# Router products token-major in step with the LayerNorm, and the first expert gather split between the first weight rows

## The reference, cut to what matters

```python
def moe_swiglu(x, w_router, b_router, wg, wu, wd):
    xt = x.reshape(B * T, D_MODEL)
    logits = (xt @ w_router).astype(jnp.float32) + b_router.astype(jnp.float32)
    vals, idx = lax.top_k(logits, TOP_K)              # TOP_K = 2 of N_EXPERTS = 8
    wts = jax.nn.softmax(vals, axis=-1)
    gate = jnp.sum(jax.nn.one_hot(idx, N_EXPERTS, dtype=jnp.float32) * wts[..., None], axis=1)
    for e in range(N_EXPERTS):                         # D_FF_EXPERT = 1408
        out = out + gate[:, e:e + 1] * swiglu(xt, wg[e], wu[e], wd[e])
```

## Time and profile before

| | us |
|---|---|
| median of three runs | 1650.25 (1649.96 to 1652.37) |
| the profiled execution | 1651.5 |
| its span, first to last instruction | 1649.7 |
| PE busy in the span | 1520.7 (92%) |
| DVE, ACT, POOL busy | 1077.6, 853.0, 555.4 |

### The profile page before, as it was taken

The page is one execution under the profiler, slowest core; times in us unless marked ns, Lnnn a source line. Parts: engine busy times, 40 slices in busy tenths (PEclk is TensorE's granted clock), DMA queues, the critical chain, the costliest instruction groups (busy, mean ns, idle before and its releaser), DMA issues. The chain is left out here.

```text
span 1649.7 us, 23014 instructions
## 1 busy us (share of the span) xinstructions
PE 1520.7 (92%) x8707; PEld 1339.8 (81%) x8707; DVE 1077.6 (65%) x1546; ACT 853.0 (52%) x1472; POOL 555.4 (34%) x336
## 2 busy tenths in 40 slices
PE   7999799999799999799998998996999999999995
PEld 6789799787699999678898988973788888888774
DVE  6779786658611011467887855777477877787784
ACT  4656555532433233355565635313566676576673
POOL 0036543000376567300555520010233343343342
PEclk9999899989899999999998998897799999999998
DMA  6322124312355455053322333125387987798780
GB/s 245 128 77 92 63 77 133 128 52 96 128 165 167 118 152 166 1 182 103 103 78 77 100 118 120 55 80 206 126 302 284 330 314 289 256 358 319 266 328 33
DMA packets 57523, 264.66 MB, mean 160 GB/s; under 512 B 9024, under 2 KB 9664, under 8 KB 48448
## 3 DMA queue, kind: packets, MB, share of 16 engines
q1 hardware_dynamic: 57408, 263.11, 45.9%
HBM read 254.54 MB, written 8.54 MB: 159 GB/s over the span
## 5 line engine op out<-in xcount | busy, mean ns | idle before, releaser
L1020 PE MATMUL ps<-Xh,Wl 128*128 128x320 f32 x976 | 332.0, 340 | 26.2 <-DVE Wl L1816 14.6
L1938 DVE TENSOR_TENSOR ml<-mraw,mh 128x1408 fp32r<-128x1408 f32 (+1 forms) x160 | 291.4, 1854 | 75.9 <-ACT mh L901 75.9
L901 ACT ACTIVATE mh<-mraw 128x1408 fp32r<-128x1408 f32 (+1 forms) x216 | 268.0, 1253 | 112.9 <-PE ps L1342 110.9
L1021 PE MATMUL ps<-Xl,Wh 128*128 128x320 f32 x976 | 312.9, 321 | 0.0
L1022 PE MATMUL ps<-Xh,Wh 128*128 128x320 f32 x976 | 312.7, 320 | 0.0
L555 POOL TENSOR_TENSOR cacc<-cacc,G 128x320 f32<-128x320 f32 x180 | 192.5, 1069 | 350.4 <-ACT G L681 334.3
L583 POOL TENSOR_TENSOR ml<-mraw,mh 128x1408 fp32r<-128x1408 f32 (+1 forms) x56 | 178.7, 3192 | 320.3 <-ACT mh L901 320.3
L1020 PEld LDWEIGHTS ps<-Xh,Wl 128*128 128x128 f32 x976 | 193.9, 199 | 50.4 <-issue 29.2
L1816 DVE TENSOR_TENSOR Wl<-raw,Wh 128x1024 fp32r<-128x1024 f32 x138 | 174.9, 1268 | 75.9 <-ACT Wh L610 74.9
L1021 PEld LDWEIGHTS ps<-Xl,Wh 128*128 128x128 f32 x976 | 194.4, 199 | 0.3
L1022 PEld LDWEIGHTS ps<-Xh,Wh 128*128 128x128 f32 x976 | 193.6, 198 | 0.0
(11 more groups left out here) (336 smaller groups left out, 2953.4 us busy)
## 6 DMA issues: line engine op xcount, KB each, us to landing
mraw<-w_moe SPq DMA_DIRECT2D x128, 704.0 KB, 6.7
raw<-w_mix SPq DMA_DIRECT2D x68, 1024.0 KB, 4.9
mraw<-w_moe SPq DMA_DIRECT2D x88, 512.0 KB, 4.7
fraw<-w_ffn SPq DMA_DIRECT2D x44, 512.0 KB, 3.5
fraw<-w_ffn SPq DMA_DIRECT2D x16, 704.0 KB, 4.0
Ss<-st_delta SPq DMA_DIRECT2D x2, 2048.0 KB, 9.4
o_delta_s<-Ss SPq DMA_DIRECT2D x8, 512.0 KB, 2.6
X<-x SPq DMA_DIRECT2D x2, 640.0 KB, 5.6
```

The costliest lines, as they stand in the source:

```text
L901: act.activation(mh[:, n % MS, 0:w], mraw[:, n % MRAW, 0:w], ACT.Copy).then_inc(m_hi, 1)
L1020: pe.matmul(out, wl, xh, start=start, stop=False)
L1021: pe.matmul(out, wh, xl, start=False, stop=False)
L1938: dve.tensor_tensor(ml[:, n % MS, 0:w], mraw[:, n % MRAW, 0:w], mh[:, n % MS, 0:w].bitcast(f32), ALU.subtract).then_inc(m_lod, 1)
```

## The change

1. **Router.** For each tile of `X`, PE makes the scores with the tile as the stationary operand, 128 tokens by 8 experts in three groups of tokens, and then turns the same tile's three groups. The copy of the scores on ACT and the turning of the scores are gone. The copies to `xth` go by halves of the width.
2. **Rests of the rows 0, 1 and 2** go to POOL (`pooled`), and `mlo(0)` to `mlo(2)` fall away on DVE.
3. **Places.** `slot` counts from 1, and `posm` is 0 where a token did not choose: the subtractions and the fill with -1 are gone, two products take the place of six instructions. PE signals the places before it makes the totals. `places` is two `tensor_tensor` comparisons for both experts of a pair, in place of six `tensor_scalar`. The flag is set after the first `places`.
4. **First gather.** The four parts of it are each gathered from `xth` and `xtl` together; two parts precede row 0, the third follows row 0 and the fourth follows row 1. `xtl` is made in two halves around `places`. `gate_weights`, the start of `acc` and `slots` move into the rows of expert 0.

```diff
         def pooled(n):
-            return n % MN in MPOOL
+            return n % MN in MPOOL or n < 3
...
             def router(l):
-                eight(wrt, PS[6], shifts(l, 2) - KT, rt_made)
...
+                for k in range(KT):
+                    pe.wait_ge(aff_done, shifts(l, 2) - KT + k + 1)
+                    for t in range(3):
+                        ins = pe.matmul(PS[7][0:rows(t), 8 * t:8 * t + 8], X[:, k, cols(t)], wrt[:, k, :],
+                                        start=(k == 0 and t == 0), stop=(k == KT - 1), skip_group_check=True)
+                    if k == KT - 1:
+                        ins.then_inc(rt_done, 1)
+                    for t in range(3):
+                        ins = pe.transpose(PS[3 * (k // 4) + t][0:rows(t), 128 * (k % 4):128 * (k % 4) + 128], X[:, k, cols(t)],
+                                           C("ident"))
+                        if k % 4 == 3:
+                            ins.then_inc(xt_mm, 1)
...
+                def gather_first(n):
...
+                    gather(PS[7 if n % 2 == 0 else 5], xth, 0, n)
+                    if n == 0:
+                        pe.wait_ge(xt_dve, 3)
+                        pe.wait_ge(flag_made, 1)
+                    gather(PS[6 if n % 2 == 0 else 4], xtl, 0, n)
+
+                gather_first(0)
+                gather_first(1)
...
+                        if not e and k < 2:
+                            gather_first(k + 2)
-                        if k == 2:
+                        if k == (2 if e else 5):
...
-                mlo(0)
-                mlo(1)
+                dve.memset(posm[:, :, :], 0.0)
                 dve.wait_ge(rt_done, 1)
...
+                x_rest(0)
                 dve.wait_ge(pos_done, 1)
...
+                dve.tensor_tensor(posm[:, 0:2, 0:NE], PS[7][:, 0:16].rearrange("p (t e) -> p t e", t=2), rk[:, 3, 0:2, :], ALU.mult)
+                link(dve.tensor_tensor(posm[0:64, 2, 0:NE], PS[7][0:64, 16:24], rk[0:64, 3, 2, :], ALU.mult))
...
-                    for t in range(3):
-                        ins = dve.tensor_scalar(Pm[:, e // 2 % 2, t, e % 2, :], C("slot"), posm[:, t, e:e + 1], None,
-                                                ALU.is_equal)
-                    ins.then_inc(m_p, 1)
+                    for t, n, r in ((0, 2, 128), (2, 1, 64)):
+                        ins = dve.tensor_tensor(
+                            Pm[0:r, e // 2 % 2, t:t + n, :, :],
+                            C("slot", r).unsqueeze(1).unsqueeze(1).broadcast_to([r, n, 2, CAP]),
+                            posm[0:r, t:t + n, e:e + 2].unsqueeze(3).broadcast_to([r, n, 2, CAP]), ALU.is_equal)
+                    ins.then_inc(m_p, 2)
...
+                    if n == 2:
+                        gate_weights()
+                    if n == 7:
+                        acc_start(l)
```

More of the change, by code:

```diff
@@ L905, in experts @@
                 for q in range(6):
-                    t, half = divmod(q, 2)
+                    half, t = divmod(q, 3)
                     act.wait_ge(xt_mm, q + 1)
@@ L913, in experts, with gathered_first @@
                 mhead(3)
[L914 to L918, removed]
+                def gathered_first(n):
+                    act.wait_ge(m_g, 2 * n + 1)
+                    act.activation(xeh[:, 0, 2 * n:2 * n + 2, :],
+                                   PS[7 if n % 2 == 0 else 5][:, :].rearrange("p (k n) -> p k n", k=2), ACT.Copy)\
                         .then_inc(m_xea, 1)
+                gathered_first(0)
+                gathered_first(1)
                 def gathered(e, n):
@@ L942, in experts @@
                         mhead(n + 3)
+                    if n in (1, 2):
+                        gathered_first(n + 1)
                     if i == MG - 1:
@@ L1275, in experts @@
                     for s in range(t + 1):
-                        pe.matmul(PS[7][0:rows(t), 8 * t:8 * t + 8],
-                                  C("upto", rows(s))[:, 0:rows(t)] if s == t else ones(rows(s), rows(t)),
-                                  rk[0:rows(s), 3, s, :], start=(s == 0), stop=(s == t))
+                        ins = pe.matmul(PS[7][0:rows(t), 8 * t:8 * t + 8],
+                                        C("upto", rows(s))[:, 0:rows(t)] if s == t else ones(rows(s), rows(t)),
+                                        rk[0:rows(s), 3, s, :], start=(s == 0), stop=(s == t))
+                ins.then_inc(pos_done, 1)
                 for s in range(3):
-                    ins = pe.matmul(PS[7][:, 32:40], ones(rows(s)), rk[0:rows(s), 3, s, :], start=(s == 0), stop=(s == 2))
+                    ins = pe.matmul(PS[6][:, 0:8], ones(rows(s)), rk[0:rows(s), 3, s, :], start=(s == 0), stop=(s == 2))
                 ins.then_inc(pos_done, 1)
@@ L1343, in wide @@
                     ins.then_inc(m_done, 1)
[L1345 to L1350, removed]
+                def gather_first(n):
+                    if n == 0:
+                        pe.wait_ge(m_p, 2)
+                        pe.wait_ge(xt_act, 3)
+                    elif n == 1:
+                        pe.wait_ge(xt_act, 6)
+                        pe.wait_ge(xt_dve, 6)
+                    else:
+                        pe.wait_ge(m_xea, n - 1)
+                        pe.wait_ge(m_xev, n - 1)
+                    gather(PS[7 if n % 2 == 0 else 5], xth, 0, n)
+                    if n == 0:
+                        pe.wait_ge(xt_dve, 3)
[3 more added lines that the diff above has]
+                gather_first(1)
                 for e in range(NE):
                     h = slice(CAP * (e % 2), CAP * (e % 2) + CAP)
-                    if e <= NE - 2:
+                    if 1 <= e <= NE - 2:
                         pe.wait_ge(m_xea, XA0 + 2 * e)
@@ L1362, in experts @@
                     for k in range(8 + SCAT):
+                        if not e and k < MG and k % 2 == 0:
+                            pe.wait_ge(m_xea, k // 2 + 1)
+                            pe.wait_ge(m_xev, k // 2 + 1)
                         if k < MG:
@@ L1896, in router @@
                 link(dve.memset(rk[:, :, :, :], 0.0))
-                mlo(0)
-                mlo(1)
+                dve.memset(posm[:, :, :], 0.0)
                 dve.wait_ge(rt_done, 1)
-                for t in range(3):
-                    ins = dve.tensor_tensor(lg[0:rows(t), t, :], PS[7][0:rows(t), 8 * t:8 * t + 8], brt[0:rows(t), :], ALU.add)
-                link(ins)
+                dve.tensor_tensor(lg[:, 0:2, :], PS[7][:, 0:16].rearrange("p (t e) -> p t e", t=2), over(brt[:, :], 2), ALU.add)
+                link(dve.tensor_tensor(lg[0:64, 2, :], PS[7][0:64, 16:24], brt[0:64, :], ALU.add))
                 le = lg.unsqueeze(3).broadcast_to([128, 3, NE, NE])
@@ L1941, in experts, with x_rest @@
             def experts(l):
-                mlo(2)
-                dve.wait_ge(pos_done, 1)
[L1945 to L1952, removed]
-                def places(e):
-                    for t in range(3):
-                        ins = dve.tensor_scalar(Pm[:, e // 2 % 2, t, e % 2, :], C("slot"), posm[:, t, e:e + 1], None,
-                                                ALU.is_equal)
-                    ins.then_inc(m_p, 1)
+                def x_rest(half):
+                    for t in range(3):
+                        q = 3 * half + t
+                        s = slice(512 * half, 512 * half + 512)
+                        dve.wait_ge(xt_act, q + 1)
+                        dve.tensor_tensor(xtl[0:rows(t), t, s], PS[q][0:rows(t), :], xth[0:rows(t), t, s].bitcast(f32),
+                                          ALU.subtract).then_inc(xt_dve, 1)
+                x_rest(0)
+                dve.wait_ge(pos_done, 1)
+                dve.tensor_tensor(posm[:, 0:2, 0:NE], PS[7][:, 0:16].rearrange("p (t e) -> p t e", t=2), rk[:, 3, 0:2, :], ALU.mult)
+                link(dve.tensor_tensor(posm[0:64, 2, 0:NE], PS[7][0:64, 16:24], rk[0:64, 3, 2, :], ALU.mult))
+                def places(e):
+                    for t, n, r in ((0, 2, 128), (2, 1, 64)):
[4 more added lines that the diff above has]
+                    ins.then_inc(m_p, 2)
                 def gathered(e, n):
@@ L1979, in experts, with gathered_first @@
                 places(0)
[L1980 to L1993, removed]
+                dve.wait_ge(pos_done, 2)
+                link(dve.tensor_reduce(rk[:, 1, 0, 0:1], PS[6][:, 0:8], AX.X, ALU.max))
+                dve.tensor_scalar(flag[:, :], rk[:, 1, 0, 0:1], CAP + 0.5, None, ALU.is_gt).then_inc(flag_made, 1)
+                x_rest(1)
+                def gathered_first(n):
+                    dve.wait_ge(m_g, 2 * n + 2)
+                    dve.tensor_copy(xel[:, 2 * n:2 * n + 2, :],
+                                    PS[6 if n % 2 == 0 else 4][:, :].rearrange("p (k n) -> p k n", k=2)).then_inc(m_xev, 1)
+                gathered_first(0)
+                gathered_first(1)
                 for n in range(MT):
```

27 lines of the change are left out of this document (8 added, 19 removed).

## The result

The changed kernel takes 1656.88 us (median of 8 runs, 1653.11 to 1662.38), the kernel before beside it 1650.96 (8 runs, 1649.05 to 1655.33): ratio 1.0038, 95% interval 1.0025 to 1.0050. It is slower by about 6 us; the forecast was 1654.0, slower by 0.23%. The profiled execution of the changed kernel took 1655.09, its span is 1653.0.

The account below looks back on a forecast made before the run. The path to the experts' stage, where PE is busy 423.62 of 430 us, was taken as the bound; 5.0 + 5.1 - 1.9 + 1.7 - 6.1 = +3.8 us on 1650.25 gave 1654.0, range 1648 to 1658.5.

Parts of the forecast that it names:

- rests on POOL under the LayerNorm: Second layer's LayerNorm tail: the two first `scaled` each wait for a POOL rest, so the router starts later, +5.0 us.
- router, from its first product to the scores: PE's new router: nine instructions a tile at clock 0.50, 1.7 us each, eight tiles 13.0 us; +5.1 us.
- from the scores to `Pm`: Choice, three `xtl` rests hiding the places, and two `posm` products take 4.7 us against 6.58: -1.9 us.
- `Pm` to the gather: Both `Pm` comparisons on DVE wait for POOL's rests of rows 2 and 3, ready after 5.6 us: +1.7 us.
- gather to row 6: Gather and first rows: row 0 raises the clock, so parts 3, 4 and row 1 run fast, 24.5 against 30.6: -6.1 us.
- a pair in the first layer: First-layer evidence: two `scaled` took 4.05 us beside two POOL rests of 4.90 us, against 1.02 undisturbed.
- The reason given for the clock: Router on PE: over 4 us idle already, 9 with the delay, so it starts at 0.50, with no reason to rise.
- the stream in the earlier trace: Nearest row for router prices: 128x128 weights, 16 columns, about 0.11 us each at 1.00, then 0.20 to 0.21 at 0.50.
- the comparison's form: `Pm` without waits: six `tensor_scalar` cost about 1.1 us, two `tensor_tensor` some 0.95, by the rows.
- The prediction's other reckoning: `Pm` by the two-elements-a-cycle rule: the new comparisons cost an estimated 0.4 us more, total about 4.3 instead of 3.8.
- the third rival: First rows: the clock does not rise in row 0, +3.8 us more, 1658; chance 0.14.
- The base: Starting time: profiled execution 1651.5 us, taken as 1.25 above the runs' median of 1650.25.

Follow-up runs that it names:

- e0_after: The changed kernel run again unedited: 1657.60 us, 1.0037 of the kernel before.
- e1: The changed kernel with the rests of rows 0 and 1 back on DVE, made while it waits for the scores: 1652.72 us.
- e8: The changed kernel with nine unused 128 by 512 products in PE's idle time ahead of the router: 1654.87 us.
- e10: The changed kernel with rests 0 and 1 on DVE, rows 2 and 3 split later, and four unused products ahead of the router: 1645.82 us.
- e4: The changed kernel with the router of before, its scores copied on ACT and turned afterwards: 1652.27 us.
- e2: The changed kernel with ACT splitting rows 2 and 3 only after moving the gather's first part: 1652.58 us.
- e6: The kernel before with the new router only: 1658.58 us, slower by 0.40%.
- e5: The changed kernel with all four parts of the first gather ahead of row 0: 1661.22 us.
- e7: The changed kernel with the old router, rests 0 and 1 on DVE, and rows 2 and 3 split later: 1640.45 us.
- e9: e7 with three unused products of 256 columns between the router and the gather: 1641.64 us.

## Why the prediction was right, point by point

The direction and the mechanisms held, that of the clock in part; the sum came out small by about 2 of 6 us. Its terms, from the dates in the table (changed, first profile, less before):

| step | forecast | measured |
|---|---|---|
| rests on POOL under the LayerNorm | +5.0 | +4.96 |
| router, from its first product to the scores | +5.1 | +5.95 |
| from the scores to `Pm` | -1.9 | -1.64 |
| `Pm` to the gather | +1.7 | +1.49 |
| gather to row 6 | -6.1 | -6.34 (-5.2 in e0_after, mean of the ten profiles that split it -5.7) |
| sum | +3.8 | +4.4 (+5.5 in e0_after) |

- **Rests on POOL under the LayerNorm.** As forecast, to 0.04 us, and e1 takes the whole of it back. What was read off a pair in the first layer carried over.
- **Router.** The term that was mis-sized: 1.80 us a tile, not 1.70, for eight tiles. Three transposes take 0.70 instead of the estimated 0.64, six score instructions 1.10 instead of 1.07, and the first tile 1.96 (1130.01 to 1131.97): over eight tiles some 0.8 us. The reason given for the clock was half of one: the clock at the start followed what stood ahead of the router (0.50 behind 9.03 us of idle time, 1.00 behind the products of e8 and e10), but the profiles of e8 and e10 show that it falls within this stream from 1.00 as well, without idle time, as the stream in the earlier trace rows did.
- **From the scores to `Pm`.** 4.94 instead of 4.7: the places (2.29 us at 0.50, 1.37 in e4 at 1.00) were not quite hidden under `xtl`, and `posm` waited 0.29 for them. This is the low clock again.
- **`Pm`.** Two waits, for row 2 and for row 3, as written (2.07 and 3.36 us for the two comparisons); e2 takes both away. The Trainium skill, page SBUF — State Buffer, section Who interferes with whom, says that a DVE instruction with two SBUF inputs contends with a GpSimd instruction that reads SBUF, that the loser waits for the whole instruction, and that a DVE instruction with one SBUF input, outside the two-port modes, does not contend. The trace agrees: `Pm` and `scaled` (two SBUF inputs) waited, the three `xtl` (one input in PSUM) took 1.87, from 1147.29 on beside POOL, and 1.87 in e2 without it. The in-place `posm` of e6 has one SBUF input and waited too; whether it ran in a two-port mode no run shows. On the comparison's form the rows were right: 1.02 us for two `tensor_tensor` (e2), 1.26 for six `tensor_scalar` (e6). The prediction's other reckoning, by the two elements a cycle that the Trainium skill, page VectorE: DVE Perf Modes, section Mode 2×_2P, gives for an fp32 `tensor_scalar` in SBUF, counted elements alone and had it the other way round.
- **Gather and first rows.** Right in the sum, with some luck. The forecast has the clock up by the end of row 0. That came in the first profile (row 0's last products take 0.34) and in two more of the ten; in seven it rose in part 3 just behind, and the term is -5.2 to -5.8 there. The 3.8 us that the third rival would have cost came in none. And the split gives only 3.4 of the gain (e5); the prediction put all to the new order.
- **What is left.** The base is 0.7: the profiled execution of before was taken for 1.25 above the median, and the median beside the changed kernel was 1650.96 instead of 1650.25. The terms give 0.6 more than forecast in the first profile, 1.7 in e0_after. From row 6 to the end the profiles take 466.4 to 467.5 us, but 468.6, 469.5 and 469.1 in the first profile of the changed kernel, in e4 and in e10. In e4 PE waits 0.37 and 1.93 us for rests of the experts' rows (at 1347.80 and 1353.85), in e10 1.64 (at 1230.41); ACT had waited for loads of `mraw` a little before, up to 1.02 us in e4 and 0.35 in e10, and four rests on DVE took 11.12 and 11.15 us beside two of POOL's. This execution of e4, 1654.44, is the slowest of its eleven. In the first profile it is the clock: 0.76 on average between 1602 and 1609, within the experts, where it is 1.00 in e0_after. Why loads or clock differ from one execution to the next wasn't tried and stays open.

## What to carry to other kernels

A rest, a copy or a compare handed to POOL is a gift only if nothing on DVE's path waits for it. Here `scaled` and `Pm`, with two SBUF inputs, waited, and so did an in-place instruction with one (e6); `xtl`, with an input in PSUM, did not. So look at what DVE does in those microseconds before counting POOL's idle time. A product form that turns few long streams into many short ones with their own weights needs a price from rows of such a stream, at the clock that it had there: here it ended at 0.50 in every profile, also where it began at 1.00, and what came behind it was slow too, which cost more than the copy and the transposition that it removed. When a change of several parts moves the time little, take it apart: here two parts worth about 11 us (e7) were hidden under two that cost about 16.

## What was not expected of the hardware

- A `tensor_scalar` with 8 columns, in place in SBUF, waited 2.5 us for POOL (e6, 2.71 against 0.17): short as it is, it ended with POOL's instruction.
- The clock fell to 0.50 while PE was busy without a gap: in the score products and transposes (e8, e10) and in the gather of 256-column products (e9). The same transposes without the score products ran at 1.00 to their end (e4, 3.20 of 3.30 us busy), and so did a gather part of 2.86 us between rows; but the score products and transposes of e10 held 1.00 for 3.8 us before it fell, so these short stretches tell no difference.
- The lower clock outlives the router: the places behind the new one take 2.29 us, behind the old one 1.37 (e4).
